# Expert matmuls with stationary weight blocks read straight from streamed slots, in place of split weights streamed past stationary tokens

## The reference, cut to what matters

```python
aff = softmax(hf @ w_router)                       # 640 x 16
gate, idx = top_k(aff.T, cap)                      # each of 16 experts takes 64 latent + 16 context tokens
xe = hf[idx]                                       # 80 x 1024 for one expert
he = silu(einsum('ecd,edf->ecf', xe, w_e1)) * einsum('ecd,edf->ecf', xe, w_e3)   # 80 x 2048
ye = einsum('ecf,efd->ecd', he, w_e2) * gate       # 80 x 1024
out = zeros.at[idx].add(ye)
```

## Time and profile before

| | |
|---|---|
| Median of three runs | 2879.96 us |
| The profiled execution's own time | 2884.09 us |
| Its span | 2882.3 us |
| TensorE matmul busy | 2545.9 us (88%) |
| TensorE weight load busy | 1914.9 us (66%) |
| VectorE busy | 1778.1 us (62%) |
| ScalarE busy | 1247.9 us (43%) |
| Mean granted TensorE clock | 0.932 |
| Read from HBM | 504.15 MB |

### The profile page before, as it was taken

How to read it: one execution, slowest core, us unless ns; L and a number is a source line. 1 busy time by engine, 2 the same in 40 slices (tenths; PEclk the granted TensorE clock), 3 DMA queues, 4 the chain that set the end, 5 groups by cost and what they waited for, 6 DMA issues and landing times. The chain is left out here.

```text
span 2882.3 us, 55324 instructions
## 1 busy us (share of the span) xinstructions
PE 2545.9 (88%) x23444; PEld 1914.9 (66%) x23444; DVE 1778.1 (62%) x1920; ACT 1247.9 (43%) x1275; POOL 445.5 (15%) x438
## 2 busy tenths in 40 slices
PE   5999995888888888888789679999999999999993
PEld 4999893777777777788544446666666666666661
DVE  2344213745736547454114578888888888888894
ACT  2212212443534424433100156666666666666671
POOL 0000000431412314314002400111110101110111
PEclk8999995998989989989799789999999999999996
DMA  8453321000000000000451199999999999999983
GB/s 316 148 196 102 119 79 54 17 11 19 12 23 19 11 18 22 11 3 10 156 198 42 64 385 373 344 372 340 367 349 371 339 372 341 372 338 372 343 323 117
DMA packets 246218, 537.95 MB, mean 187 GB/s; under 512 B 13254, under 2 KB 53926, under 8 KB 245752
## 3 DMA queue, kind: packets, MB, share of 16 engines
q1 hardware_dynamic: 242936, 524.39, 49.3%
q0 software_dynamic: 3072, 10.49, 1.6%
HBM read 504.15 MB, written 30.70 MB: 186 GB/s over the span
## 5 line engine op out<-in xcount | busy, mean ns | idle before, releaser
L1724 DVE TENSOR_TENSOR w_lo<-w_raw,w_hi 128x4096 fp32r<-128x4096 f32 x192 | 866.9, 4521 | 116.7 <-ACT w_hi L1564 116.6
L1564 ACT ACTIVATE w_hi<-w_raw 128x4096 fp32r<-128x4096 f32 x192 | 695.6, 3623 | 126.7 <-PE ps_y L1663 87.8
L1661 PE MATMUL ps_h<-w_hi,xT_hi 128*80 128x512 f32 x1024 | 413.1, 403 | 34.7 <-DVE xT_lo L1755 26.8
L1662 PE MATMUL ps_h<-w_lo,xT_hi 128*80 128x512 f32 x1024 | 408.3, 399 | 0.0
L1663 PE MATMUL ps_h<-w_hi,xT_lo 128*80 128x512 f32 x1024 | 407.8, 398 | 0.0
L1661 PEld LDWEIGHTS ps_h<-w_hi,xT_hi 128*80 128x80 f32 x1024 | 154.3, 151 | 119.9 <-DVE xT_lo L1755 25.7
L1661 PE MATMUL ps_y<-w_hi,hiddenT_hi 128*80 128x512 f32 x512 | 204.6, 400 | 14.1 <-DVE hiddenT_lo L1782 14.1
L1663 PEld LDWEIGHTS ps_h<-w_hi,xT_lo 128*80 128x80 f32 x1024 | 154.4, 151 | 87.9 <-issue 4.7
L1662 PEld LDWEIGHTS ps_h<-w_lo,xT_hi 128*80 128x80 f32 x1024 | 154.6, 151 | 81.2 <-issue 4.2
L1662 PE MATMUL ps_y<-w_lo,hiddenT_hi 128*80 128x512 f32 x512 | 201.6, 394 | 0.0
L1663 PE MATMUL ps_y<-w_hi,hiddenT_lo 128*80 128x512 f32 x512 | 201.4, 393 | 0.0
(11 more groups left out here) (282 smaller groups left out, 4045.4 us busy)
## 6 DMA issues: line engine op xcount, KB each, us to landing
w_raw<-in_w_e SPq DMA_DIRECT2D x192, 2048.0 KB, 8.7
w_ada<-in_w_ada SPq DMA_DIRECT2D x6, 4096.0 KB, 18.0
w_in_raw<-in_w_in SPq DMA_DIRECT2D x23, 1024.0 KB, 6.2
rkv_scratch<-projected SPq DMA_DIRECT2D x24, 320.0 KB, 6.4
rkv_T<-rkv_scratch SPq DMA_DIRECT2D x8, 960.0 KB, 5.4
gates_scratch<-projected SPq DMA_DIRECT2D x16, 320.0 KB, 6.6
gate_sb<-gates_scratch SPq DMA_DIRECT2D x8, 640.0 KB, 6.4
x<-in_x_sample SPq DMA_DIRECT2D x8, 512.0 KB, 6.4
```

The lines of the kernel that those rows point to most:

```text
L1564: act.activation(high_of[w][:, :, :], raw[w][s % 2][:, :, :], ACT.Copy).then_inc(s_hi[w], 1)
L1661: pe.matmul(out, x[0][:, k, :], w[0][:, k, ks], start=first, stop=False, skip_group_check=True)
L1662: pe.matmul(out, x[0][:, k, :], w[1][:, k, ks], start=False, stop=False, skip_group_check=True)
L1724: v.tensor_tensor(low_of[w][s % 2][:, :, :], raw[w][s % 2][:, :, :], high_of[w][:, :, :], ALU.subtract).then_inc(s_lo[w], 1)
```

## The change: what it does

- The split is gone: no `high`, no `low`, no float32r tiles. TensorE reads the landed weights as plain float32.
- The operands are swapped: a 128x128 block of weights is stationary, and 80 token columns are streamed past it. One half expert (1024 hidden features) has for `w_e1` and `w_e3` 8 x 8 such blocks each and for `w_e2` another 64.
- The result comes out with features on partitions. Hidden needs no turning before `output`; instead the 80x1024 result of each expert is turned back by eight transposes (`turn_y`), after ScalarE has copied it out of PSUM (`copied`). VectorE applies gate and modulation in one instruction per half (`gated`); GpSimd only issues the indirect DMAs.
- The weights land in a ring of eight slots of 2 MiB, in the order of use: 24 pieces in a round of two experts. A load waits until the piece eight before it is used.
- The hidden features of a half are numbered so that partition p of tile m stands for feature 8p + m. A partition's eight rows of `w_e2` lie together in DRAM (four of them, 16 KB, in one piece). The price is that a block of `w_e1` or `w_e3` takes every eighth column of its slot: `w[:, q, f:FH:FK]`, 128 columns with a step of 8 elements (32 bytes). A partition of these pieces is filled with 4 KB runs.

The core of the diff:

```diff
-            def split_product(out, x, w, k, ks, first, last_):
-
-                pe.matmul(out, x[0][:, k, :], w[0][:, k, ks], start=first, stop=False, skip_group_check=True)
-                pe.matmul(out, x[0][:, k, :], w[1][:, k, ks], start=False, stop=False, skip_group_check=True)
-                return pe.matmul(out, x[1][:, k, :], w[0][:, k, ks], start=False, stop=last_, skip_group_check=True)
+            def hidden(i, s, kh):
+
+                x = xT[s // 2]
+                if kh == 0 and s % 2 == 0:
+                    pe.wait_ge(s_xt, 4 * i + s + 2)
+                for n, (ps, free) in enumerate(((ps1, s_h1), (ps3, s_hh))):
+                    p = STEP * s + 2 * kh + n
+                    if kh == 0 and (s or not at_zero(i)):
+                        pe.wait_ge(free, 4 * i + s)
+                    landed(pe, i, p)
+                    pe.sem_inc(s_pe_turn, 1)
+                    w = raw[p % NBUF]
+                    for f in range(FK):
+                        for q in range(KQ):
+                            k = KQ * kh + q
+                            last = pe.matmul(tile_of(ps, f), w[:, q, f:FH:FK], x[:, k, :], start=(k == 0 and f % PER == 0),
+                                             stop=(k == KD - 1), skip_group_check=True)
+                    last.then_inc(s_used, 1)
...
+                    w = raw[(p + a) % NBUF]
+                    for m in range(KN):
+                        for q in range(KQ):
+                            f = KQ * a + q
+                            last = pe.matmul(tile_of(psY, m), w[:, q, m * P:(m + 1) * P], hT[s % 2][:, f, :],
+                                             start=(hf == 0 and f == 0 and m % PER == 0), stop=(hf == 1 and f == FK - 1), skip_group_check=True)
+                    last.then_inc(s_used, 1)
...
             def body(i, first, last):
...
+                for s in range(4):
+                    prev = (i, s - 1) if s else None if first else (i - 1, 3)
+                    done = (i, 0) if s == 3 else (i - 1, 1) if s == 1 and not first else None
+                    hidden(i, s, 0)
                     if s < 2:
                         turn_x(i, 2 + s)
+                    if s == 2 and not last:
+                        slots(i + 1)
+                    if s == 3 and not last:
+                        turn_x(i + 1, 0)
+                    if done:
+                        turn_y(*done, 0)
+                    hidden(i, s, 1)
+                    if s == 3 and not last:
+                        turn_x(i + 1, 1)
+                    if done:
+                        turn_y(*done, 1)
+                    if prev:
+                        output(*prev)
...
+            def gate_up(i, s):
+
+                v.wait_ge(s_sg, 4 * i + s + 1)
+                v.tensor_tensor(split(hT[s % 2]), split(sg), banked(ps1), ALU.mult).then_inc(s_h1, 1)
                 v.drain()
+                consumed(v, i, STEP * s + 3)
+                v.tensor_tensor(split(hT[s % 2]), split(hT[s % 2]), banked(ps3), ALU.mult).then_inc(s_hh, 1)
+
+            def gated(i, j, b):
+
+                cs = slice(b * 512, (b + 1) * 512)
+                v.wait_ge(s_ytr, 4 * i + 2 * j + b + 1)
+                if b == 0:
+                    if not at_zero(i):
+                        v.wait_ge(s_out[j], 16 * i)
+                    v.tensor_copy(row[j][:, :], gt[j][:, 1:2])
+                v.scalar_tensor_tensor(ye[j][:, cs], psT[0:CAP, :], gt[j][:, 0:1], g2row[:, cs], ALU.mult, ALU.mult).then_inc(s_ye, 1)
```

More of the change, by code:

```diff
@@ L1475, in expert_phase @@
         sem = lambda n: ctx.enter_context(nc.semaphore(n))
[L1476 to L1481, removed]
+        raw = [sb(f"w_piece{b}", [P, KQ, DM]) for b in range(NBUF)]
         iota, tokid = sb("iota_slot_sb", [P, CAP]), sb("tok_id_sb", [P, NT])
@@ L1524, in _ @@
[L1524 to L1531, removed]
@@ new lines, in consts @@
+            def consts():
+                sp.dma_start(iota[:, :], d["iota_slot"]).then_inc(s_cst, 16)
+                sp.dma_start(tokid[:, :], d["tok_id"]).then_inc(s_cst, 16)
+                for j, rows in enumerate((A, B)):
+                    sp.dma_start(g2row[rows, :], d["mod"][j:j + 1, G2:G2 + DM].to_broadcast([rows.stop - rows.start, DM])).then_inc(s_g2, 16)
+            def body(i, first, last):
+                for p in range(ROUND):
+                    if first and p in (4, 5):
+                        continue
+                    if not first or p >= NBUF:
+                        consumed(sp, i, p - NBUF)
+                        sp.sem_inc(s_turn, 1)
+                    load(i, p)
@@ L1549, in _ @@
+            consts()
             rounds(sp, body)
+            for p in (4, 5):
+                consumed(sp, NR, p - NBUF)
+                load(NR, p)
             sp.wait_ge(s_xt, 4 * NR)
@@ L1592, in _, with sigmoid, copied @@
-            high(W1, 0, 0)
-            high(W3, 0, 0)
+            def sigmoid(i, s):
+                consumed(act, i, STEP * s + 2)
+                act.activation(split(sg), banked(ps1), ACT.Sigmoid).then_inc(s_sg, 1)
+            def copied(i, j):
+                n = 2 * i + j
+                if j == 1 and isinstance(i, int) and i == NR - 1:
+                    act.wait_ge(s_used, ROUND * NR)
+                else:
+                    consumed(act, i, (2 * j + 3) * STEP - 1)
+                if j == 1 or not at_zero(i):
+                    act.wait_ge(s_ytr, 2 * n)
+                act.activation(split(yT), banked(psY), ACT.Copy).then_inc(s_yc, 1)
@@ L1696, in body @@
-            def body(i, first, last):
-                for s in range(NST):
-                    before = (i, s - 1) if s else None if first else (i - 1, NST - 1)
-                    hidden(W1, i, s)
-                    if before:
-                        turn(*before)
-                    hidden(W3, i, s)
-                    if s == FQ and not last:
-                        slots(i + 1)
+            def hidden(i, s, kh):
[15 more added lines that the diff above has]
+                    last.then_inc(s_used, 1)
@@ new lines, in output @@
+            def output(i, s):
+                p = STEP * (s + 1) + 4
+                hf, n = s % 2, 2 * i + s // 2
+                pe.wait_ge(s_hh, 4 * i + s + 1)
+                if hf == 0 and (s or not at_zero(i)):
+                    pe.wait_ge(s_yc, n)
+                for a in range(2):
+                    if s == 3:
+                        landed(pe, i + 1, p - ROUND + a)
+                    else:
+                        landed(pe, i, p + a)
+                    pe.sem_inc(s_pe_turn, 1)
+                    w = raw[(p + a) % NBUF]
[5 more added lines that the diff above has]
+                    last.then_inc(s_used, 1)
@@ L1705, in body @@
                     if s < 2:
                         turn_x(i, 2 + s)
-                    if s >= NST - 2 and not last:
-                        turn_x(i + 1, s - NST + 2)
-                    if before:
-                        output(*before)
+                    if s == 2 and not last:
[5 more added lines that the diff above has]
+                    hidden(i, s, 1)
@@ L1715, in _ @@
             rounds(pe, body)
[L1716 to L1717 removed]
+            output(NR - 1, 3)
+            for b in range(2):
+                turn_y(NR - 1, 1, b)
         @block.vector
         def _(v):
[L1721 to L1724 removed]
             def select(n):
```

234 lines of the change are left out of this document (90 added, 144 removed).

## The result

The changed kernel takes 4594.27 us (median of 4 runs, 4591.56 to 4596.77) against 2879.4 for the kernel before. The ratio is 1.597 [1.594, 1.600]: 60% slower, where the prediction said 6% slower and gave a range up to 3340.

A forecast was written before the change was run, and what follows sets the result against it. TensorE's stream was taken to bound the kernel. Start 1670.5, 3 for half clock, 1311 matmuls, 10 searches, 8 and 13 turnings give 3015.5; with the tail, a 3055.8 us span, 173.5 over before: 3053 us, range 3000 to 3340.

The forecast's parts named there:

- What bounds the kernel before: Expert phase: TensorE's stream is the wall, 1062 of 1165 us; waits on VectorE are 34.7 and 14.1 us.
- Direction: Expert matmuls: many short streams limited by 128-column weight loads replace three long streams, 1311 us against 1062, losing 249 us.
- The clock: Rival for the expert matmuls: granted clock falls to 1.2 GHz, 213 ns a record, 4359 us in all; chance 0.03.
- 3 us lost to the half clock: Start of the expert phase: TensorE starts at 1670.5 and loses 3 us at the half clock.
- Strided weights at no cost: w_e1 and w_e3 blocks, 8192 records: reading every eighth column was taken to add nothing to the load.
- its rival: Strided loads in w_e1 and w_e3 take 213 instead of 107 ns: 873 us more, 3926 us; chance 0.11.
- The pace of 106.7 ns: Expert matmuls: each of 12288 records takes 106.7 ns, set by the 128-column weight load, 1311 us together.
- Faster by a hidden load: Rival: expert weight loads are hidden, streams at 67 ns and then DMA set the pace, about 2750 us; chance 0.06.
- New waits: Single hidden accumulators and turn_y: TensorE's waits on VectorE and ScalarE are covered by other matmuls and cost nothing.
- transfers: Expert weights: TensorE asks for 307 GB/s, DMA has shown 361 to 411, so longer DRAM runs give nothing.
- start: First expert matmul at 1670.5 instead of 1676.0, since the wait for VectorE's first subtraction is gone.
- tail: After the last matmul: 4.0 us to the last indirect DMA instead of 4.7, 40.3 us in all.

The follow-up runs named there:

- e8: Kernel before, with VectorE taking the turned token rows from PSUM before, not behind, its subtraction for the next w_e3 block at a round's end: 2831.7 us, ratio 0.984.
- e3: Changed kernel with contiguous weight blocks (old numbering of hidden features) and 128 streamed columns, 48 of them zeros: 3144.5 us, ratio 1.095.
- e6: e3 with 112 streamed columns in place of 128, blocks contiguous: 3139.8 us, ratio 1.091.
- e2: Changed kernel with the old numbering of hidden features, so contiguous weight blocks, still 80 streamed columns: 4386.5 us, ratio 1.527.
- e5: e2 with 24 dense matmuls of 512 columns ahead of the first round: two runs, 4165.7 and 4336.1 us.
- e1: Changed kernel, blocks still strided, with 128 streamed columns, 48 of them zeros: 4175.0 us, ratio 1.453.
- e4: Changed kernel, strided and 80 columns, with 24 dense matmuls of 512 columns ahead of the first round: 4609.6 us, ratio 1.605.
- e12: e5 with eight more dense matmuls of 512 columns behind each slot search: 3679.5 us, ratio 1.278.

## Why the prediction was wrong

- **What bounds the kernel before:** right, and e8 bears it out: taking the waits away moves the time by 1.6%, against a full stream. (Of VectorE's 174.63 us in the earlier trace rows the subtractions are 150, so not nearly all.)
- **Direction:** right, and for the reason given. Many short streams behind loads of 128 columns are more work than three long streams; at full clock and contiguous this gives 3144 (e3) and 3140 (e6) against the forecast's 3053.
- **The clock, the step that failed:** the rival "The clock" had 0.03, on the argument that the columns "fill 67 of 107 ns, not 13". The row behind it showed a TensorE that does not stop in this stream and whose clock falls; no row shows the clock of a long stretch of 80 columns, so the case was open, and an argument is not worth the 0.97 that I gave it. And it asked only what takes a clock down. The expert phase begins in a gap at 1.2 GHz (the earlier trace rows has 0.50 at 1670), and 80 columns do not lift it (e2), though with contiguous blocks they held it for 263 us (e5). Price, contiguous: 4387 - 3140 = 1247 us; by the records, 12288 x (213 - 112) ns = 1241. The "3 us lost to the half clock" of the start became the whole phase.
- **Strided weights at no cost, the second failure:** a strided load takes 239 ns at either clock, 2.1 times the contiguous one at full clock. The slack that was argued from the float32r stream was that of another operand and says nothing on a load. Because the clock was down anyway, the stride added only 4594 - 4387 = 208 us (8192 x 26 ns = 213); with the clock up it would be 4175 - 3145 = 1030 us (8192 x 127 ns = 1040). Either failure hides most of the other, so undoing one alone from the changed kernel (e1: 419 us, e2: 208) shows much less than both together (1450). Each alone puts the time above the range (4387 and 4175). Only one step was run, so whether 32 bytes matter or any step would do is open. The line rule of the Trainium skill ("SBUF — State Buffer", "Specifications (TRN2)") speaks of full bandwidth only from two hits per 16-byte line; the measured 239 against 112 ns agrees in direction and nearly in the doubling that its rival was priced at (213 against 107).
- **The pace of 106.7 ns:** 112 measured, 12288 x 5 ns = 61 us. In the earlier trace rows I took starts of matmul groups with different shapes, and these do not follow their loads at one distance: 1602.46 is 0.11 us behind its load and 1604.16 is 0.03. The loads' own starts give the right one, and so do: 15 loads in 1.68 us are 112 ns, if no record is assumed missing. In the trace of before, weight loads at the router:

```profile
1602.35 1.87 PEld L1346 LDWEIGHTS ps_merge<-w_router_sb,w_merge 128*128 128x128 f32 x16
1604.13 0.30 PEld L1331 LDWEIGHTS ps_merge<-w_out_sb,mergedT 128*128 128x128 f32 x2
```

  (1604.13 - 1602.35) / 16 = 111 ns.
- **Pauses at the loop's jumps, which the sum does not have:** right for the changed kernel at its slow pace (0.42 us at most), wrong by 19.5 us in e3, where the records come every 112 ns.
- **Faster by a hidden load:** it did not come. The pace is 112 ns even at full clock, above the 92.5 below which it would decide.
- **New waits, transfers, start, tail:** right. Once its first matmul has started, TensorE waits for no other engine until the tail; 145 GB/s asked for where 411 were to be had.

The sum of what was missed, by the records: 1241 (clock) + 213 (stride at that clock) + 61 (pace) = 1515 of 1541 us. How clock and stride share it depends on the order: with the stride taken at full clock it has 1030 us, and the clock 4594 - 4175 = 419. The other 26 us are the small groups at 1.2 GHz. A slot search takes 2.18 us and not 1.38, a turning of gathered rows 0.53 and not 0.28, one of the result 0.85 and not 0.44 (the changed kernel from 2120 on, against e5 at full clock): 7 x 0.80 + 32 x 0.25 + 30 x 0.41 = 26 us.

## What to carry over

Before operands are swapped so that weights become stationary, count what TensorE streams between two loads: if the load is the limit, the engine can look 100% busy and yet run at half its clock, so find in a trace a stretch with that width and see which clock it rises to from cold, not only whether it keeps one. A weight block is read contiguously; a layout that helps DRAM by a few per cent is not bought with a step on the operand that already sets the pace. And when two suspected costs can hide each other, run both undone as well as each alone.

## What the runs showed of the hardware that was not expected

- With 128 contiguous float32 weight columns to load, records that stream 80 to 128 columns come every 112 ns at 2.4 GHz, and with 80 columns every 213 at 1.2. With a step of 32 bytes it is 239 ns at both.
- With 80 float32 columns behind each contiguous load the clock has memory: up if it was up (263 us in e5), down if it was down (2.7 ms in e2), at 100% busy TensorE in both. With 112 and 128 columns it rose by itself (e6, e3), with 128 even past strided blocks (e1). With 80 columns past strided blocks it fell within 7 us of full clock (e4).
- At the jump of the loop over rounds TensorE pauses for 3.1 to 4.8 us when the last 128 records ahead of it were 112 ns each (e1, e3, e6, e12), and for 0.42 us at most when they were 213 (the changed kernel, e2, e5). What it waits for no trace says.
